# Prompt attention of a hybrid decoder layer: where the per-head query and key weights are kept, one NeuronCore

## What is computed

```python
x <- LN1(alpha*x + 0.5*SwiGLU_a(x))
x <- LN2(alpha*x + W_out[MLA(x) ; RWKV7(x)])
x <- LN3(alpha*x + 0.5*SwiGLU_b(x))

q = einsum('bsc,chd->bshd', rmsnorm(c_q), w_uq)        # 8 heads, 64 + 32 columns each
q_nope, q_rope = q[..., :64], rope(q[..., 64:])
o_lat = attend(q_nope with w_uk, q_rope, ckv, k_rope)  # prompt: causal; samples: paged cache of 2048
y_mla = einsum('bshr,rhv->bshv', o_lat, w_uv)
```

## Time and profile before

| | |
|---|---|
| median of 3 executions | 2396.45 us (2394.7 to 2397.5) |
| the profiled execution, its own time | 2406.32 us |
| span of its profile | 2403.9 us |
| TensorE busy | 2297.0 us (96%) |
| VectorE, ScalarE, GpSimd busy | 1578.7, 1026.2, 457.9 us |
| mean granted TensorE clock | 0.981 |
| first and last piece of prompt attention | 996.1 and 1179.4 us from the start |

### The profile page before, as it was taken

How to read it: one execution, slowest core, us unless ns; L and a number is a source line. 1 busy time by engine, 2 the same in 40 slices (tenths; PEclk the granted TensorE clock), 3 DMA queues, 4 the chain that set the end, 5 groups by cost and what they waited for, 6 DMA issues and landing times.

```text
span 2403.9 us, 52287 instructions
## 1 busy us (share of the span) xinstructions
PE 2297.0 (96%) x21030; PEld 2033.0 (85%) x21030; DVE 1578.7 (66%) x2680; ACT 1026.2 (43%) x1839; POOL 457.9 (19%) x452
## 2 busy tenths in 40 slices
PE   7999999999999999997898999998899999999997
PEld 7999999988887788754567888787899999998886
DVE  7777766665686756765544565656787766666577
ACT  6333333354444756543343344433433333345452
POOL 4232200000034211011110122345233210000005
PEclk9999999999999999999999999898999999999999
DMA  4465532377555444533332122345355643349653
GB/s 162 144 215 190 187 103 94 126 254 276 175 195 162 121 121 116 153 67 66 65 85 106 29 74 63 113 159 175 117 194 173 220 138 100 120 142 316 206 174 110
DMA packets 322226, 348.74 MB, mean 145 GB/s; under 512 B 49441, under 2 KB 220274, under 8 KB 321218
## 3 DMA queue, kind: packets, MB, share of 16 engines
q1 hardware_dynamic: 259298, 286.86, 37.8%
q10 hardware_dynamic: 60576, 53.65, 6.5%
q0 software_dynamic: 2112, 4.89, 0.8%
HBM read 246.36 MB, written 98.44 MB: 143 GB/s over the span
## 4 chain that ended last, share of the span: by engine, by line
PE 75%; DVE 7%; SPq 6%; issue 6%; ACT 3%; DMA 1%; POOL 1%; ACTq 0%; POOLq 0%; DVEq 0%
PE ps_b L763 19%; PE ps_a L763 18%; PE ps_a L470 7%; PE ps_b L470 6%; PE ps_pj L1541 4%; PE ps_wo L4059 4%; PE ps_rk L3237 4%; PE ps_pj L1523 2%; SPq L2697 2%; SPq L2694 1%; SPq L2695 1%; PE ps_rk L3333 1%; PE ps_rk L3247 1%; PE ps_rk L3385 1%; PE ps_rk L3233 1%
## 5 line engine op out<-in xcount | busy, mean ns | idle before, releaser
L763 PE MATMUL ps_b<-X_b,W_b 128*128 128x272 f32 x3696 | 466.5, 289 | 8.3 <-DVE X_b L1036 7.6
L763 PEld LDWEIGHTS ps_b<-X_b,W_b 128*128 128x128 f32 x3696 | 465.6, 189 | 9.3 <-DVE X_b L1036 7.9
L763 PE MATMUL ps_a<-X_a,W_a 128*128 128x272 f32 x3696 | 466.5, 289 | 7.2 <-DVE X_a L1036 4.7
L763 PEld LDWEIGHTS ps_a<-X_a,W_a 128*128 128x128 f32 x3696 | 464.9, 189 | 8.8 <-DVE X_a L1036 4.9
L470 PE MATMUL ps_a<-W_a,H_a 128*128 128x512 f32 x924 | 216.8, 391 | 0.0
L470 PE MATMUL ps_b<-W_b,H_b 128*128 128x512 f32 x924 | 214.8, 389 | 1.0 <-DVE H_b L1122 1.0
L470 PEld LDWEIGHTS ps_b<-W_b,H_b 128*128 128x128 f32 x924 | 173.3, 188 | 37.4 <-DVE W_b L1075 1.4
L470 PEld LDWEIGHTS ps_a<-W_a,H_a 128*128 128x128 f32 x924 | 174.3, 189 | 36.2
L844 ACT ACTIVATE W_a<-wraw_a 128x512 fp32r<-128x512 f32 x154 | 95.8, 629 | 164.2 <-PE ps_a L763 65.0
L844 ACT ACTIVATE W_b<-wraw_b 128x512 fp32r<-128x512 f32 x154 | 95.8, 629 | 163.3 <-PE ps_b L763 64.9
L1075 DVE TENSOR_TENSOR W_b<-wraw_b,W_b 128x512 fp32r<-128x512 f32 x154 | 118.5, 775 | 69.4 <-ACT W_b L844 69.4
(11 more groups left out here) (525 smaller groups left out, 4166.6 us busy)
## 6 DMA issues: line engine op xcount, KB each, us to landing
hraw_a<-hidden SPq DMA_DIRECT2D x77, 256.0 KB, 3.8
hraw_b<-hidden SPq DMA_DIRECT2D x77, 256.0 KB, 3.7
wraw_pj<-in_w_in SPq DMA_DIRECT2D x28, 512.0 KB, 3.8
wraw_a<-in_ffa_w_gate SPq DMA_DIRECT2D x22, 512.0 KB, 4.7
wraw_a<-in_ffa_w_up SPq DMA_DIRECT2D x22, 512.0 KB, 4.9
hraw_a<-in_ffa_w_down SPq DMA_DIRECT2D x22, 512.0 KB, 5.5
down_sums<-hraw_a SPq DMA_DIRECT2D x11, 1024.0 KB, 6.5
wraw_a<-down_sums SPq DMA_DIRECT2D x44, 256.0 KB, 2.9
```

The source lines that it names most:

```text
L763: last = nc.tensor.matmul(ps[:, bank + p, :PIECE], W[:, n % WC, wp, k * P:(k + 1) * P], operand(i, xp)[:, k, p * PIECE:(p + 1) * PIECE], s ...
```

## The change

The sample queries' weight tile `wq_si` gets 128 columns a head in place of 96: the two swapped rotary halves are stored with it, as in `wq_pi`. A tile `wk_si` for all of `w_uk` is added. `load_constants` fills them once. Heads 0 and 1 still read `wq_pi` and `wk_pi`; heads 2 to 7 read the shared tiles and wait for `si_consts_in` instead of the head's own load. The 24 DMAs of the loads of heads 2 to 7 are gone, and with them the waits of SP between batches 0 to 5 of the pages. Tiles allocated behind these move by 4 KB in each partition, and a wait for the earlier stage's row stores is added on ScalarE ahead of its first copy into `yb`.

```diff
+        def norms_stored(self, eng):
+            for s in range(2):
+                eng.wait_ge(nrm_out[s].h, nrm_out[s].at(32 * (5 - s)))
...
-            for h in range(H - 2):
-                sp.wait_ge(pc_done.h, pc_done.at(h * NPC + NPC))
-                first.load(sp, h + 2, h % 2)
-                inputs.load_pages(sp, h)
+            sp.wait_ge(pc_done.h, pc_done.at(NPC))
+            for b in range(H - 2):
+                inputs.load_pages(sp, b)
             inputs.load_new(sp)
...
-                if j == 0:
-                    pe.wait_ge(w_in[u].h, w_in[u].at((h - u) * 32 + 64))
+                if j == 0 and h < 2:
+                    pe.wait_ge(w_in[u].h, w_in[u].at(64))
+                elif j == 0:
+                    pe.wait_ge(I.consts_in.h, I.consts_in.at(I.CONSTS))
...
-                        last = nc.tensor.matmul(ps[:, 7, :], wq[:, u, a, :], lat[:, a, c], start=(a == 0), stop=(a == 1))
+                        w = wq[:, u, a, :] if h < 2 else I.wq[:, a, h, :]
+                        last = nc.tensor.matmul(ps[:, 7, :], w, lat[:, a, c], start=(a == 0), stop=(a == 1))
                 else:
+                    w = wk[:, u, :] if h < 2 else I.wk[:, h * HD:(h + 1) * HD]
...
                 act.wait_ge(o_done.h, o_done.at(h * NQP + m + 1))
+                if h == 0 and m == 0:
+                    before.norms_stored(act)
...
-        self.wq, self.wukT, self.wv = sb("wq", [P, 2, H * (HD + ROPE)]), sb("wukT", [HD, H, P]), sb("wv", [P, RW])
+        self.wq, self.wukT, self.wv = sb("wq", [P, 2, H, P]), sb("wukT", [HD, H, P]), sb("wv", [P, RW])
+        self.wk = sb("wk", [P, RW])
...
+    CONSTS = (6 + 7) * 16
+
     def load_constants(self, sp):
         A = self.A
         sp.dma_start(self.pages[:], A["page_table"]).then_inc(self.table_in.h, 16)
-        for dst, src in ((self.wq[:], A["w_uq"].rearrange("(a p) c -> p a c", p=P)),
+        QD, HR = HD + ROPE, ROPE // 2
+        uq = A["w_uq"].rearrange("(a p) (h c) -> p a h c", p=P, h=H)
+        for a in range(2):
+            for to, cols in ((slice(0, QD), slice(0, QD)), (slice(QD, QD + HR), slice(HD + HR, QD)), (slice(QD + HR, P), slice(HD, HD + HR))):
+                sp.dma_start(self.wq[:, a, :, to], uq[:, a, :, cols]).then_inc(self.consts_in.h, 16)
+        for dst, src in ((self.wk[:], A["w_uk"]),
```

More of the change, by code:

```diff
@@ L2281, in piece @@
                     for a in range(2):
-                        last = nc.tensor.matmul(ps[:, 7, :], wq[:, u, a, :], lat[:, a, c], start=(a == 0), stop=(a == 1))
+                        w = wq[:, u, a, :] if h < 2 else I.wq[:, a, h, :]
+                        last = nc.tensor.matmul(ps[:, 7, :], w, lat[:, a, c], start=(a == 0), stop=(a == 1))
                 else:
+                    w = wk[:, u, :] if h < 2 else I.wk[:, h * HD:(h + 1) * HD]
                     for c in range(2):
-                        last = nc.tensor.matmul(ps[c * HD:(c + 1) * HD, 7, :], wk[:, u, :], lat[:, 2, c * 512:(c + 1) * 512], start=True,
+                        last = nc.tensor.matmul(ps[c * HD:(c + 1) * HD, 7, :], w, lat[:, 2, c * 512:(c + 1) * 512], start=True,
                                                 stop=True, tile_position=(0, c * HD), skip_group_check=True)
@@ L2348, in queries @@
             def queries():
-                pe.wait_ge(I.consts_in.h, I.consts_in.at(7 * 16))
+                pe.wait_ge(I.consts_in.h, I.consts_in.at(I.CONSTS))
                 for a in range(2):
-                    w = I.wq[:, a].rearrange("p (j s c) -> p s j c", s=2, c=QD)
+                    w = I.wq[:, a, :, :QD].rearrange("p (j s) c -> p s j c", s=2)
                     for s in range(2):
@@ L2542, in rope_queries @@
             def rope_queries():
-                dve.wait_ge(I.consts_in.h, I.consts_in.at(7 * 16))
+                dve.wait_ge(I.consts_in.h, I.consts_in.at(I.CONSTS))
                 dve.wait_ge(I.q_copied.h, I.q_copied.at(1))
@@ L2712, in mla_sample @@
         wv, causal8, ck, kr, qr4, qlT, nk, Pn = I.wv, I.causal8, I.ck, I.kr, I.qr4, I.qlT, I.nk, I.Pn
-        sb("gap", [P, 3104])
+        sb("gap", [P, 2080])
         ckT = sb("ckT", [P, 2, 2, PAST])
```

## The result

The changed kernel takes 2381.06 us, median of 6 runs (2371.87 to 2384.53), against 2395.80 us of the kernel before, run beside it (6 runs, 2394.66 to 2398.95): ratio 0.9925, 95% interval 0.9911 to 0.9939. By the ratio the gain is 18.0 us (14.6 to 21.3), by the two medians 14.7 us, where 22.1 were forecast; the time is 6.7 us above the 2374.4 forecast and lies in the range given. The two profiled executions differ by more, 2403.9 - 2377.7 = 26.2 us of span, and the question behind the experiments is which of these numbers is the change.

What follows compares the result with a forecast made beforehand. SP's queue, filled by page loads, was taken to make the weights of heads 5 to 7 late. Terms -23.7 + 1.6 = -22.1 us took 2396.45 to 2374.4 us, range 2370.5 to 2383.

Steps and rivals of the forecast that it cites:

- The heads' waits go: Heads 2 to 7 on TensorE: each falls to 23.59 us without load waits and lower clock, saving 23.7 us.
- The constants: SP's constant loads grow from 7 to 13 DMAs at 0.50 us an issue, 3.0 us in; landing costs 0.
- The upper bound of 1.27 us an issue: Six added issues on SP at the price seen behind large stores, adding 4.6 us; wait at pair 3 up to 6.2.
- The last page: SP's last page load: issued until 1243.3 instead of 1253.25 us, landing at 1245.6.
- What is late next: First turn of pair 3, `turn_pages(3)`: TensorE waits about 1.6 us for the last page, bounds 0 to 6.2.
- Rival 1: SP's queue binds more: added issues stall, wait at `turn_pages(3)` 5 to 8 us; gain 14.5, about 2382 us; chance 0.20.
- Rival 2: Pages for pair 3 not late at all: gain 23.7 plus up to 1.11 us, 2371.6 to 2372.8 us; chance 0.08.
- At nothing: TensorE's products, ScalarE's added row-store wait and the recurrence's first load cost nothing; that load keeps 24 us of room.
- rival 3: Short-run constants land slowly, at 1060 us; head 2 stands 30 us; time 2406 us, slower than before; chance 0.04.
- The first three cases: Gains of 20 to 24 us (chance 0.62), over 24 (0.08) and 10 to 20 (0.20), all counted as faster.
- the prediction's own bound of 4.8 us: Whole-kernel time: smallest change that can be told from none, about 0.2%.
- rival 4: Row sums, zero fill or output stores hold heads 5 to 7 near 30 us; time 2392 to 2396 us; chance 0.04.

Runs made afterwards that it cites:

- six long ones: Changed kernel with query weights laid out wide in DRAM, still six DMAs, each of 128 long runs; 2381.67 us, ratio 0.9936.
- twelve short-run loads: Changed kernel with the six short-run DMAs of the query weights issued a second time into unused room; 2383.90 us, ratio 0.9952.
- wide layout: Changed kernel with query weights laid out at 128 columns a head in DRAM, one DMA of 256 4 KB runs replacing six; 2380.80 us, ratio 0.9925.
- loads on ScalarE: Kernel before, with the loads of heads 2 to 7 issued by ScalarE instead of SP, same DMAs and buffers; 2378.70 us, ratio 0.9917.

## Why the prediction was right, and where it was off

**The heads' waits go.** Right in the place and in the mechanism: 23.59 us a head, full clock, `queries()` at 1170.1 where 1171.4 was forecast, the stage having begun 1.34 us earlier. Off in the size: the term of 23.7 us was one execution's. Other executions of the kernel before give S to Q 192.6 and 193.6 us, which with 175.3 us of the changed kernel makes 17.3 and 18.3 us. This is the step that failed: I treated the row spacings of a single profile as the kernel's, although that execution was 10 us above its own median, and I put this distance wholly outside the stage. At least 5.4 of its 10 us lay inside it. The term of 23.7 us is 19.7 in the mean of the three profiles.

**The constants.** The step "an issue beside its like takes 0.50 us, so 3.0 us in" failed. The issues I took it from have 256 runs or fewer; with 1024 runs it is 0.97 us in the mean, and `wk_si` behind them took 1.38. First constant to first page is 12.2 us instead of 7.2 - 2.0 = 5.2: about 6.9 us in, not 3.0. The upper bound of 1.27 us an issue held it, but its reason was queueing behind large stores, and six long ones in the same place took 0.45 us each. The short runs are the reason, and the issues do stall behind each other for them, as `wk_si` shows.

**The last page.** Forecast as issued until 1243.3, it was issued until 1244.1, and the agreement is partly luck: 3.9 us more for the constants were met by 1.3 us of earlier start and by page issues that lost less to stretches. The forecast that they follow each other without a gap was wrong. 128 pages at 1.62 us are 207 us; they took 226.4 and 219.3 in its two profiles. The last page landed 1.79 us after its issue began, at 1245.57 us, where the sum had it at 1245.6.

**What is late next.** Right: `turn_pages(3)`, and nothing else. 1.6 us forecast, 2.81 and 0 us in the two profiles. With the clock behind the wait and a later copy counted, Q to R is 4.0 and 0.4 us above the 97.94 of the kernel before. Rival 1 named issues dearer than 0.50 us and stalled behind each other, and both are there, but its wait of 5 to 8 us is not. Rival 2's mechanism, no wait at all, is what the second profile shows. So the forecast and rival 2 are not two cases but one that differs between executions. That the measured gain (18.0 us by the ratio, 14.7 by the medians) falls among rival 1's 10 to 20 us, and the time beside its 2382, is chance: rival 1 took 9.2 us off at pair 3 from a full 23.7, and the runs have about 2 us off there from 19.7.

**At nothing.** Row stores, short-run landings, the recurrence's first load: no wait for any appeared. The weights among the constants landed in medians of 3.6 to 4.8 us from their issue, far from rival 3's 10.68 each, and even twelve short-run loads did not hold head 2. The rule of the Trainium skill's page "DMA: Bandwidth & Descriptors" ("Specifications", "Rules for kernel authors") against runs below 512 B and many small transfers did not show in landings late enough to matter: the two long-run loads of the query weights landed in medians of 5.2 us (one DMA) and 2.9 us (six). What the short runs cost was issue time on SP, of which that rule does not speak. The Trainium skill's page "Perfetto Trace Analysis" ("DMA Instruction — HWDGE (DVE, Sync)") says that the time shown for such an instruction covers a wait for a lock, the generation of its descriptors and the setting of its semaphore, and not the movement of the data; that the six issues take 2.72 us with 128 runs each and 5.83 with 1024 agrees with it.

**The sum.** Where the prediction has -23.7 + 1.6 = -22.1 us, the profiles have -19.7 in the heads and +2.2 from Q to R, mean against mean: a gain of 293.0 - 275.5 = 17.5 us for the stage. The ratios give 18.0 us (14.6 to 21.3) and 15.1 us (11.0 to 19.2). So the stage accounts for the change within these intervals, and no loss behind it shows. Of the 26.2 us between the first two spans, 19.6 are the stage (some 6 of them the slow heads of that one execution), 5.8 the recurrence and 1.3 what lies ahead, less 0.5 behind W; the last three are no larger than these parts differ among the other profiles. In the recurrence it is the low-clock stretches that differ. Runs of 2 us windows with a granted clock under 0.97 begin at 1464, 1532 and 1546 us in the first profile of before, and at 1512 and 1522 after. Counted from R that is 171, 239 and 253 us against 240 and 250: two of them stand at nearly the same places of the program, and the first is missing after. Which of these places has a stretch, and how long, changes from execution to execution. My estimate of their cost, the time of each window times one less its clock, is 10.3 us before and 5.1 us after, so 5.2 of the 5.8 us; over all twelve profiles it is 1.7 to 10.3 us.

**A slip in the chances.** The first three cases that are faster have 0.62 + 0.08 + 0.20 = 0.90. By the prediction's own bound of 4.8 us all of rival 4 (2392 to 2396 us) counts as the same, so with half of the rest "faster" should have had 0.91 and not 0.92, and half of rival 4 does not belong in it.

**Left open.** What stretches SP's page issues. Some of it is regular: in all five profiles of the two kernels a spacing of 1.9 to 2.6 us instead of 1.62 comes at the 12th, 26th and 40th page and then about every 14th, nine in all, mostly 1.9 to 2.1, and one more of 2.6 to 3.6 us is `load_new`'s. The others, of 2 to 4.7 us (those with a head's load in them aside), mostly lie in other places each time. They meet a DMA issue of ScalarE or GpSimd no more often than any spacing does (3 to 6 of the 12 to 22 above 2.05 us in a profile, against 35 or 36 of all 127). The cause of either kind is not known. Open is also whether wide layout or loads on ScalarE beat the changed kernel: their stage is 0.2 to 4.1 us shorter, and their ratios lie within the intervals of each other.

## What to carry to other kernels

When a load is late, look at what stands ahead of it in its queue before making it disappear: the heads' loads were 12 us of a queue that page issues filled for 207 us and more, and moving either off it gave the whole gain. Count issues by what issues of as many runs take in the trace, the issue behind them included, and follow the queue to the next reader, because a delay in a queue that stays the bound is paid there nearly one for one. Where the wait to be removed is a small difference of two long sums, as here 30 us of issues against 23.6 us of computing, take its size from several profiles: it varied between 17 and 24 us in three.

## What the runs showed of the hardware

- A DMA's issue on SP took 0.45 us with 128 long runs (six in a row, mean) and 0.97 us with 1024 short ones, with the bytes in all the same; one of 256 runs of 4 KB took 0.38 us.
- The price of short runs is partly paid by the next issue: `wk_si` took 1.38 and 1.33 us behind six short-run DMAs in the changed kernel's two profiles, 0.43 us behind six long ones and 0.46 us behind one.
- The same loads issued by ScalarE (24 of them) did not slow the heads: 23.58 us each. The Trainium skill's page "DMA: Bandwidth & Descriptors" ("Issuing engines are not separate DMA queues") says that issuing on several engines saves only the time in which the sequencer starts the DMA, which is usually small beside the DMA itself. It is so here for one DMA (0.50 us for an issue, 2.2 to 2.8 us to landing), but summed over a queue that time was the bound, and saving 12 us of it was worth as much as the whole change.
- Of 127 page spacings in SP's queue, 82 to 91 were 1.6 us in the five profiles of the two kernels. Nine of the longer ones, mostly 1.9 to 2.1 us, stood about every 14th page in all five; the others reached 4.7 us, mostly in other places each time. First page to last differed by 8 us between executions of one program (239.2 and 231.1 us).
- The recurrence, whose code is the same in every kernel here, took in the twelve profiles 257.3 to 265.1 us, and the lower clock in it cost 1.7 to 10.3 us by my estimate above.
